# Attention probabilities divided ahead of the value product, which is turned round and packed in two column halves

## The chip, the cores and the metric

The kernel runs on one core of one Trainium2 chip. The metric is the device time of one execution in microseconds (us). Engines are TensorE (PE; PEld is its weight load), VectorE (DVE), ScalarE (ACT), GpSimd (POOL) and SyncE (SP, which issues the loads). All data are 32-bit floats. A product of the program shows as two passes in the trace, a turning (a transpose through TensorE) as one.

## What is computed

Two layers of a trunk on 384 tokens: 128 context tokens and 256 latent ones. A layer has three mixers that read one projection of the normalised tokens (latent attention, a gated linear scan, a state-space scan), whose gated sum is projected back, and a mixture of experts. The part that matters here is the attention of 16 heads and its output projection:

```python
def attend(q, k, v):
    ...
        s = jnp.einsum('bqhd,bkhd->bhqk', qblk, k).astype(jnp.float32) * scale
        p = jax.nn.softmax(s, axis=-1).astype(v.dtype)
        return jnp.einsum('bhqk,bkhd->bqhd', p, v)
...
    o_a = attend(q, k, v).reshape(Bsz, L, A_HEADS * A_V) @ P['a_wo'][l]
...
    merged = g[:, :, 0] * o_a + g[:, :, 1] * o_b + g[:, :, 2] * o_c
```

Context tokens read context keys alone; latent tokens read latent and context keys. Queries and keys have 96 columns per head, values 64.

## The kernel before, in words

Everything is written by hand: each engine has its own instruction list in a block, semaphores order them, and a block ends when all engines have ended theirs. The layer loop runs twice over the same blocks. The tokens are three tiles of 128; tile 0 is the context, tiles 1 and 2 are latent.

The attention block (TensorE code from line 846) goes through 48 steps, step i being head i // 3 and token tile i % 3. Tile 0 has one key tile, tiles 1 and 2 have three, so a step is 128 or 384 columns wide. A step is: scores on TensorE (line 873), the negated row maximum on VectorE (967), the exponential with its row sum on ScalarE (928), the turning of the probabilities on TensorE, one pass per key tile (882), their copy out of PSUM by VectorE (945), and the weighing of the values on TensorE (301, called from `weigh_values`), with the turned probabilities as weights and 64 value columns moving. Once per head, TensorE turns the queries and keys of the head after next (863, seven passes), ScalarE copies the queries (913) and VectorE the keys (938). Scores run AHEAD = 2 steps ahead of the turning; the probabilities have three buffers. Five PSUM banks rotate among scores, turned probabilities, queries and keys; three more collect the weighed values of eight heads per tile. After eight heads VectorE takes reciprocals of the row sums and scales the values out of PSUM (952, 954) into `o_tok`, tokens on partitions.

The next block makes the gate of this mixer (`W_GA`) and the output projection (`W_AO`). The projection needs features on partitions, so TensorE turns `o_tok` in 24 passes (`to_features`, line 333), VectorE copies it (497) into `oT`, and only then `feature_major` (301) runs. `gated_sum` multiplies the projection by the gate and writes the result to `mT`. Between these stand products of the modulation (380 in four quarters of the array's columns, 405 its small follow-up). Weight chunks pass through a ring of three, each loaded when the chunk three ahead of it has been read last. The block behind it begins the linear scan; there VectorE copies six decay tiles out of PSUM (1184).

What sets the order is the order of the lines below, engine by engine.

## Time and profile before

| what | value |
|---|---|
| median of three runs | 2664.28 us (2662.90 to 2666.83) |
| the profiled execution | 2660.27 us |
| its span, first to last instruction | 2658.3 us |
| TensorE busy | 2324.3 us, 87% of the span |
| VectorE busy | 828.9 us, 31% |
| ScalarE busy | 565.8 us, 21% |
| mean granted TensorE clock | 0.932 of full speed |

The busy shares are averages over stages with different limits, and matmuls are pipelined, so a busy TensorE is not one at its peak. A stage is read from its own stretch: who waits for whom there, and what a single head does in order of time. The attention stages begin at 229.4 and 1546.8 us.

### The profile page before, as it was taken

The numbers are of one execution on the slowest core, as the hardware profiler recorded it, in microseconds if no ns is written. First come the engines' busy times: TensorE is split into PE (matmuls) and PEld (weight loads), VectorE is DVE, ScalarE is ACT, GpSimd is POOL, SyncE is SP. The second block draws the span as 40 slices with busy tenths as digits, with TensorE's granted clock in tenths as the row PEclk, the third lists the DMA queues.
The fourth block names the chain that finished last, engine by engine and source line by source line (L and its number), as shares of the span: only waits on it lengthen the run. The fifth ranks groups of instructions, "written<-read, shape, count | busy, mean of one in ns | idle before, by whom it ended". The sixth has DMA issues, their size and how long they took to land. (4 is left out here: it accounts for less than half of the span.)

```text
span 2658.3 us, 35179 instructions
## 1 busy us (share of the span) xinstructions
PE 2324.3 (87%) x14554; PEld 1406.2 (53%) x14554; DVE 828.9 (31%) x1447; ACT 565.8 (21%) x1160; POOL 96.5 (4%) x64
## 2 busy tenths in 40 slices
PE   6999999999887988988479999999998779799873
PEld 3546754754555545555335466547545555455542
DVE  1255512530635222110203653125206452321002
ACT  2133301410244121000021332033102540210000
POOL 0000000100021000000000000001000210000000
PEclk8999998999988998998789999989999889899996
DMA  6321052214301215999553211331243102179993
GB/s 252 111 97 64 1 190 80 79 64 158 127 20 45 95 38 218 402 419 420 219 212 112 81 56 50 141 111 48 89 143 132 48 1 94 38 282 413 420 420 134
DMA packets 136274, 407.01 MB, mean 153 GB/s; under 512 B 9446, under 2 KB 34534, under 8 KB 125352
## 3 DMA queue, kind: packets, MB, share of 16 engines
q1 hardware_dynamic: 122600, 388.37, 38.4%
q10 hardware_dynamic: 11776, 9.97, 1.1%
q0 software_dynamic: 1728, 6.29, 0.7%
q8 instruction: 120, 1.97, 0.3%
q14 instruction: 50, 0.41, 0.0%
HBM read 388.59 MB, written 16.02 MB: 152 GB/s over the span
## 5 line engine op out<-in xcount | busy, mean ns | idle before, releaser
L301 PE MATMUL ps<-hT,ring 128*128 128x384 f32 x1344 | 473.3, 513 | 57.7 <-ACT arena L1524 30.6
L301 PEld LDWEIGHTS ps<-hT,ring 128*128 128x128 f32 x1344 | 268.0, 202 | 251.3 <-issue 84.1
L301 PE MATMUL ps<-ring,hT 128*128 128x512 f32 x768 | 337.1, 600 | 3.9 <-PEq L1033 3.9
L301 PE MATMUL ps<-arena,ring 128*128 128x384 f32 x768 | 253.0, 492 | 11.4 <-DVE arena L499 5.1
L301 PEld LDWEIGHTS ps<-ring,hT 128*128 128x128 f32 x768 | 147.1, 193 | 192.2 <-issue 191.6
L301 PEld LDWEIGHTS ps<-arena,ring 128*128 128x128 f32 x768 | 146.9, 192 | 115.4 <-issue 17.2
L1807 PE MATMUL ps<-ring,arena 128*32 128x256 f32 x2432 | 147.4, 405 | 30.3 <-DMA ring<-in_e_w 25.8
L1807 PE MATMUL ps<-arena 128*32 128x256 f32 x2432 | 143.9, 398 | 25.9 <-DMA arena<-in_e_w 25.9
L333 PE MATMUL ps<-cst,arena 128*128 128x128 f32 x472 | 77.6, 313 | 75.0 <-DVE arena L2086 34.4
L1807 PEld LDWEIGHTS ps<-ring,arena 128*32 128x32 f32 x2432 | 89.2, 117 | 85.0 <-issue 38.5
L1807 PEld LDWEIGHTS ps<-arena 128*32 128x32 f32 x2432 | 86.6, 115 | 78.7 <-issue 36.5
L2068 DVE TENSOR_TENSOR arena<-ps,arena 128x256 f32<-128x256 f32 (+1 forms) x44 | 17.1, 389 | 326.0 <-ACT arena L1917 326.0
L301 PE MATMUL ps<-ring,arena 128*128 128x384 f32 (+1 forms) x320 | 117.5, 528 | 0.0
L333 PEld LDWEIGHTS ps<-cst,arena 128*128 128x128 f32 x472 | 61.9, 160 | 102.4 <-DVE arena L2086 36.9
L301 PE MATMUL ps<-arena 128*128 128x64 f32 (+1 forms) x608 | 97.7, 295 | 1.5 <-DVE arena L945 1.4
L301 PEld LDWEIGHTS ps<-arena 128*128 128x128 f32 x608 | 87.8, 191 | 12.2 <-DVE arena L945 5.6
L301 PEld LDWEIGHTS ps<-ring,arena 128*128 128x128 f32 x320 | 60.6, 190 | 55.5 <-issue 30.6
L301 PE MATMUL ps<-mT,ring 128*128 128x384 f32 x256 | 83.1, 487 | 3.0 <-DVE arena L1665 3.0
L1917 ACT ACTIVATE arena<-ps 128x256 f32<-128x256 f32 (+1 forms) x44 | 15.7, 356 | 319.9 <-PE ps L1807 319.9
L301 PE MATMUL ps<-arena,mT 128*128 128x384 f32 x192 | 66.3, 509 | 15.7 <-DVE arena L2020 15.7
L1524 ACT ACTIVATE arena<-ps,arena 128x128 f32<-128x128 f32 x192 | 54.5, 366 | 73.2 <-DVE arena L1580 67.6
L1830 PE MATMUL ps<-arena 128*32 128x256 f32 x1216 | 68.8, 379 | 1.0 <-DVE arena L2077 1.0
(293 smaller groups left out, 2456.4 us busy)
## 6 DMA issues: line engine op xcount, KB each, us to landing
ring<-in_e_w SPq DMA_DIRECT2D x48, 2048.0 KB, 15.9
arena<-in_e_w SPq DMA_DIRECT2D x48, 2048.0 KB, 17.5
ring<-in_w_in SPq DMA_DIRECT2D x36, 2048.0 KB, 7.8
ring<-in_w_ada SPq DMA_DIRECT2D x24, 2048.0 KB, 8.1
ring<-in_a_wo SPq DMA_DIRECT2D x4, 2048.0 KB, 11.6
ring<-in_b_wo SPq DMA_DIRECT2D x4, 2048.0 KB, 8.1
ring<-in_c_wo SPq DMA_DIRECT2D x4, 2048.0 KB, 8.0
ring<-in_w_out SPq DMA_DIRECT2D x4, 2048.0 KB, 7.7
```

What stands on the lines that cost most here:

```text
L301: ins = pe.matmul(out, a, b, start=(i == 0), stop=(i == len(pairs) - 1))
L333: ins = pe.transpose(out[0:s.shape[1], i * P:i * P + P], s, ident)
L1524: ins = act.activation(diff[:, q % 2, P * i:P * i + P], bank(("ai", s, q))[:, P * i:P * i + P], ACT.Relu, bias=ex2[:, d, 0, h:h + 1], scal ...
L1807: ins = pe.matmul(out[32 * g:32 * g + 32], hc[:, e % 2, k, 32 * r:32 * r + 32], w[:, :, k, P * g:P * g + P], start=(k == 0), stop=(k == KD ...
L1830: ins = pe.matmul(out[32 * g:32 * g + 32], hidT[:, e % 2, r, 32 * k:32 * k + 32], w2[:, k, 256 * g:256 * g + 256], start=(k == 0), stop=(k ...
L1917: act.activation(sil[:, 2 * b:2 * b + n, :], bank(("w13", e, b))[:, 0:256 * n].rearrange("p (r i n) -> p r i n", i=2, n=P)[:, :, 0, :], AC ...
L2068: dve.tensor_tensor(hid[:, 2 * b:2 * b + n, :], bank(("w13", e, b))[:, 0:256 * n].rearrange("p (r i n) -> p r i n", i=2, n=P)[:, :, 1, :], ...
```

## The change

It does the following.

- The probabilities are divided by their row sum as soon as the exponential is done: VectorE takes the reciprocal of one column and multiplies the step's probabilities in place (`share_out`). TensorE's turning waits for that (`shared_out`).
- The copy of the turned probabilities moves from VectorE to ScalarE (`turned`), behind the exponential of three steps later and, once per head, the query copy. It goes to a buffer of three heads, in which the two latent tiles of one key tile lie side by side.
- The weighing is turned round: values are the weights (64 columns), turned probabilities move (128 columns for the context tile, 256 for both latent ones). Two heads go to columns 0 to 63 and 64 to 127 of the array. It is done once per pair of heads, behind the turning of the next pair's first step.
- A pair's result is copied once (`heads_out`) into `mT`, features on partitions already. So the turning of `o_tok` and its copies go, and the output projection reads `mT`. Its gated sum goes to `gated_a`, which VectorE copies to `mT` at the head of the next block.
- Scores run three steps ahead, probabilities have four buffers (two in `wsm`, which is not read any more at that time), six banks rotate, two hold pairs. The row sums and maxima lie in `rstd`.
- In the projection block, one small modulation product moves behind the first half of the output projection.

```diff
-            AHEAD = 2
-            B_PV, N_ROT = 5, 5
+            AHEAD = 3
+            B_PV, N_ROT, N_PV = 6, 6, 2
...
                     def turn_probs(i):
...
-                        pe.wait_ge(*read(("s", i)))
+                        pe.wait_ge(*following(pe, "shared_out"))
...
+                    def weigh_values(j):
+
+                        out = claim(pe, ("pv", j), B_PV + j % N_PV)
+                        for h in (2 * j, 2 * j + 1):
+                            for t in range(NT):
+                                pe.wait_ge(*read(("pt", NT * h + t)))
+                        for c in range(2):
+                            h = 2 * j + c
+                            pe.matmul(out[V_A * c:V_A * c + V_A, 0:P], v_a[:, 0, h, :], probsT[:, h % 3, 0:P], start=True, stop=True)
+                        for k in range(NKT - 1):
+                            for c in range(2):
+                                h = 2 * j + c
+                                ins = pe.matmul(out[V_A * c:V_A * c + V_A, P:T], v_a[:, 1 + k, h, :],
+                                                probsT[:, h % 3, P + 2 * P * k:P + 2 * P * (k + 1)],
+                                                start=(k == 0), stop=(k == NKT - 2))
+                        ins.then_inc(*makes(("pv", j)))
...
-                        if i >= 1:
-                            weigh_values(i - 1)
+                        if i >= 1 and i % (2 * NT) == 0:
+                            weigh_values(i // (2 * NT) - 1)
...
                         if j >= 0 and next_head(j):
                             queries(next_head(j))
+                        if j >= 0:
+                            turned(j)
...
+                    def share_out(i):
...
+                        dve.wait_ge(*read(("s", i)))
+                        r = rsum[:, t, h:h + 1]
+                        dve.reciprocal(r, r).then_inc(*counts("dve_step"))
+                        dve.wait_ge(*counted("dve_step"))
+                        dve.tensor_scalar(probs[i % 4][:, 0:n], probs[i % 4][:, 0:n], r, None, ALU.mult
+                                          ).then_inc(*counts("shared_out"))
...
-                    to_features(pe, "oa", o_tok)
+                    feature_major(pe, W_AO[0], ("ao", 0), mT)
                     modulation_features_pe(pe, ADA_FIRST + 1, rows_a[:, 1, :])
-                    project_pe(pe, W_AO, "ao", oT, "oa", lambda: modulation_pe(pe, ADA_FIRST + 2))
+                    modulation_pe(pe, ADA_FIRST + 2)
+                    feature_major(pe, W_AO[1], ("ao", 1), mT)
...
                 def _(dve):
+                    dve.tensor_copy(mT[:, :, :], gated_a).then_inc(*counts("dve_step"))
+                    dve.wait_ge(*counted("dve_step"))
```

On TensorE, in the middle of the attention, before. L873 are scores, L882 the turning of probabilities, L301 the weighing; a `psum_free` wait is for a reader of that PSUM bank.

```order
L882 MATMUL ps<-cst,arena 128x128 x2
L301 MATMUL ps<-arena 128x64 [waits psum_free0,psum_free6]
L301 MATMUL ps<-arena 128x64 x2
L873 MATMUL ps<-arena 128x384 [waits psum_free0]
L882 MATMUL ps<-cst,arena 128x128 [waits psum_free1,psum_free4]
L301 MATMUL ps<-arena 128x64 [waits psum_free4,psum_free7]
L301 MATMUL ps<-arena 128x64 x2
L873 MATMUL ps<-arena 128x128 [waits psum_free2,psum_free3]
```

Now, on TensorE at a pair's end. L893 and L897 are the weighing, in 64-column weights.

```order
L882 MATMUL ps<-cst,arena 128x128 [waits psum_free5,shared_out]
L882 MATMUL ps<-cst,arena 128x128 x2
L873 MATMUL ps<-arena 128x128 [waits psum_free0,psum_free4,psum_free3]
L882 MATMUL ps<-cst,wsm 128x128 [waits psum_free1,shared_out]
L893 MATMUL ps<-arena 64x128 [waits psum_free5,psum_free3,psum_free1,psum_free6]
L893 MATMUL ps<-arena 64x128
L897 MATMUL ps<-arena 64x256 x6
L873 MATMUL ps<-arena 128x384 [waits psum_free2]
```

The weighing of single steps has become one group per pair, and its first product waits for the readers of several banks, which are the copies of the turned probabilities; the next scores stand behind it.

On ScalarE at the same places, before. L928 is the exponential, L913 the query copy.

```order
L928 ACTIVATE arena<-ps,arena 128x384 [waits nmax_ready,psum_full4,psum_full3,psum_free2]
L913 ACTIVATE arena<-ps 96x384 [waits psum_full0,psum_free4]
L928 ACTIVATE arena<-ps,arena 128x384 [waits nmax_ready,psum_full3,psum_full2,psum_free0]
L928 ACTIVATE arena<-ps,arena 128x128 [waits nmax_ready,psum_full0,psum_full4,psum_free3]
L928 ACTIVATE arena<-ps,arena 128x384 [waits nmax_ready,psum_full2,psum_full1,psum_free0]
```

Now, on ScalarE. L947 is the exponential, L918 the query copy, L933 the copy of turned probabilities.

```order
L947 ACTIVATE arena,rstd<-ps,rstd 128x384 [waits psum_full2,nmax_ready,psum_full1]
L918 ACTIVATE arena<-ps 96x384 [waits psum_full3,psum_free2]
L933 ACTIVATE arena<-ps 128x3x128 [waits psum_full5,psum_free3]
L947 ACTIVATE arena,rstd<-ps,rstd 128x128 [waits psum_full0,nmax_ready,psum_full5]
L933 ACTIVATE arena<-ps 128x128 [waits psum_full1,psum_free0]
```

Each step's copy stands behind the exponential of the step three later, and at a head's end behind the query copy too; the exponential waits for VectorE's maximum (`nmax_ready`).

On VectorE, now, where a pair's output copy (L974) stands. L986 is the maximum, L967 and L969 the dividing, L959 the keys' copy.

```order
L967 RECIPROCAL rstd<-rstd 128x1 [waits psum_free0]
L969 TENSOR_SCALAR arena<-arena,rstd 128x128 [waits dve_step]
L974 COPY mT<-ps 128x384 [waits psum_full6]
L986 TENSOR_REDUCE rstd<-ps 128x1 [waits psum_full4,psum_free6]
L959 COPY arena<-ps 96x512 [waits psum_full0]
L967 RECIPROCAL rstd<-rstd 128x1 [waits psum_free2,psum_free0]
L969 TENSOR_SCALAR wsm<-wsm,rstd 128x384 [waits dve_step]
L986 TENSOR_REDUCE rstd<-ps 128x1 [waits psum_full2]
```

The copies of turned probabilities are gone from this engine; each step has a maximum and a dividing, one step behind it.

## Rows read from the trace of the kernel before

**Rows 1.** Waits, first attention stage: who waited, us, times, longest.

```profile
ACT arena L928 <- DVE arena L967: 34.7, 32, 1.8
DVE arena L967 <- PE ps L873: 14.8, 40, 0.6
```

**Rows 2.** Windows: length, busy PE, PEld, DVE, ACT, POOL, granted clock, DMA.

```profile
240.00:268.40 28.40, 28.40 (x209) 24.22 (x209) 20.84 (x44) 14.36 (x46) 0.00 (x0) 1.00 0.01 2
...
306.00:310.00 4.00, 1.69 (x14) 1.41 (x12) 3.13 (x7) 0.00 (x0) 0.00 (x0) 0.78 0.01 2
...
532.00:534.00 2.00, 0.10 (x1) 0.00 (x0) 2.00 (x2) 1.35 (x2) 2.00 (x1) 1.00 0.00 0
```

**Rows 3.** Timeline, one head of the attention: start, length, engine, line, operation.

```profile
263.07 0.86 PE L873 MATMUL ps<-arena 96*128 96x384 f32 x2
...
263.77 0.93 PE L863 MATMUL ps<-cst,arena 128*96 128x128 f32 x7
...
264.04 0.56 DVE L967 TENSOR_REDUCE arena<-ps 128x1 f32<-128x384 f32 x1 [0.38 <-PE ps L873]
...
264.77 0.58 ACT L928 ACTIVATE arena<-ps,arena 128x384 f32<-128x384 f32 x1 [1.01 <-DVE arena L967]
264.86 0.78 PE L301 MATMUL ps<-arena 128*128 128x64 f32 x6
...
265.47 0.49 ACT L913 ACTIVATE arena<-ps 96x384 f32<-96x384 f32 x1
265.48 0.86 PE L873 MATMUL ps<-arena 96*128 96x384 f32 x2
...
267.46 0.29 DVE L967 TENSOR_REDUCE arena<-ps 128x1 f32<-128x128 f32 x1 [0.25 <-PE ps L873]
...
268.39 0.93 PE L863 MATMUL ps<-cst,arena 128*96 128x128 f32 x7
```

**Rows 4.** Timeline, first and last instructions of the first attention stage.

```profile
229.42 1.70 PE L863 MATMUL ps<-cst,arena 128*96 128x128 f32 x14 [1.16 <-PEq L598]
...
234.12 0.33 PE L882 MATMUL ps<-cst,arena 128*128 128x128 f32 x1 [1.18 <-ACT arena L928]
...
309.42 0.69 DVE L954 TENSOR_TENSOR mT<-ps,arena 128x512 f32<-128x512 f32 x1
...
310.80 23.01 PE L301 MATMUL ps<-hT,ring 128*128 128x384 f32 x64 [2.64 <-PEq L846]
```

**Rows 5.** VectorE's groups by shape: count, busy us, mean ns, idle before.

```profile
L945 DVE COPY arena<-ps 128x384 f32<-128x384 f32 x64 | 35.7, 557 | 3.9 <-PE ps L882 2.9
...
L938 DVE COPY arena<-ps 96x512 f32<-96x512 f32 x32 | 22.0, 686 | 38.3 <-PE ps L863 34.4
...
L1403 DVE TENSOR_SCALAR arena<-arena,vec 128x388 f32<-128x388 f32 x24 | 10.2, 423 | 15.0 <-ACT arena L1365 14.5
...
L1184 DVE COPY arena<-ps 128x512 f32<-128x512 f32 x12 | 8.3, 692 | 13.8 <-PE ps L1038 13.8
...
L369 DVE TENSOR_SCALAR hT<-hT,amp,mod 128x128 f32<-128x128 f32 x12 | 4.1, 344 | 0.1
...
L1189 DVE TENSOR_SCALAR arena<-arena 128x3072 f32<-128x3072 f32 x2 | 3.5, 1759 | 0.1
...
L952 DVE RECIPROCAL arena<-arena 128x8 f32<-128x8 f32 x12 | 2.4, 203 | 0.4
```

**Rows 6.** Timeline of TensorE in the experts: products in four column quarters.

```profile
1046.45 10.57 PE L1807 MATMUL ps<-ring,arena 128*32 128x256 f32 x192 [2.41 <-DVE arena L2034]
```

**Rows 7.** Timeline of TensorE between gate and output projection.

```profile
356.33 0.95 PE L405 MATMUL ps<-fold,arena 128*128 128x2 f32 x8
...
357.21 1.92 PE L380 MATMUL ps<-ring,scond 128*32 128x512 f32 x16
...
359.07 2.84 PE L333 MATMUL ps<-cst,mT 128*128 128x128 f32 x24
...
364.67 20.88 PE L301 MATMUL ps<-arena,ring 128*128 128x384 f32 x64 [1.98 <-DVE arena L497]
```

More of the change, by code:

```diff
@@ L878, in turn_probs @@
                         k0, k1 = KEYS[t]
-                        pe.wait_ge(*read(("s", i)))
+                        pe.wait_ge(*following(pe, "shared_out"))
                         out = rotating(("pt", i))
                         for k in range(k1 - k0):
-                            ins = pe.transpose(out[:, P * k:P * k + P], probs[:, i % 3, P * k:P * k + P], ident)
+                            ins = pe.transpose(out[:, P * k:P * k + P], probs[i % 4][:, P * k:P * k + P], ident)
                         ins.then_inc(*makes(("pt", i)))
-                    def weigh_values(i):
-                        h, t = STEPS[i]
-                        k0, k1 = KEYS[t]
-                        if h % 8 == 0:
-                            claim(pe, ("pv", t, h // 8), B_PV + t)
-                        pe.wait_ge(*read(("pt", i)))
-                        c = V_A * (h % 8)
-                        ins = matmuls(pe, ps[:, B_PV + t, c:c + V_A],
-                                      [(probsT[:, i % 2, P * k:P * k + P], v_a[:, k0 + k, h, :]) for k in range(k1 - k0)])
-                        if h % 8 == 7:
-                            ins.then_inc(*makes(("pv", t, h // 8)))
+                    def weigh_values(j):
[13 more added lines that the diff above has]
+                        ins.then_inc(*makes(("pv", j)))
                     head(0)
@@ L914, in queries, with turned @@
                         act.wait_ge(*read(("qT", h)))
+                    def turned(i):
+                        h, t = STEPS[i]
+                        n = KEYS[t][1] - KEYS[t][0]
+                        act.wait_ge(*made(("pt", i)))
+                        if t == 0 and h >= 3:
+                            act.wait_ge(*made(("pv", (h - 3) // 2)))
+                        if t == 0:
+                            out = probsT[:, h % 3, 0:P]
+                            src = bank(("pt", i))[:, 0:P]
+                        else:
+                            out = probsT[:, h % 3, P:].rearrange("p (k q) -> p k q", q=2 * P)[:, :, P * (t - 1):P * t]
+                            src = quad(bank(("pt", i))[:, 0:T])
+                        act.activation(out, src, ACT.Copy).then_inc(*reads(("pt", i)))
                     queries(0)
@@ L970, in _ @@
                             keys(next_head(j))
-                        if 0 <= j < len(STEPS):
-                            turned(j)
-                        if j >= 2:
-                            h, t = STEPS[j - 2]
-                            if h % 8 == 7:
-                                heads_out(t, h // 8)
+                        if 0 <= j + AHEAD - 1 < len(STEPS):
+                            share_out(j + AHEAD - 1)
+                        if j >= 1 and (j - 1) % (2 * NT) == 0:
+                            heads_out((j - 1) // (2 * NT) - 1) if j > 1 else None
             with nc.Block() as block:
```

45 lines of the change are left out of this document (19 added, 26 removed).

## The prediction

> **What bounds the kernel now.** I read the waits of the attention stretch first, then its busy times by window, then the instructions of one head in order of time. In the waits, ScalarE waits for VectorE and VectorE for TensorE, while TensorE hardly waits for anybody [rows 1]. The window of the steady part says the same: TensorE is busy for all of its 28.4 us, VectorE for 20.84, ScalarE for 14.36, at full granted clock [rows 2]. One head (three steps) takes from the start of its seven turning passes at 263.77 us to the next such start at 268.39 us, 4.62 us, and in it TensorE goes from pass to pass [rows 3]; a pair of heads is 9.24 us. The stage takes from 229.42 to 310.80 us, 81.4 us [rows 4], twice in the run (once per layer). So only what shortens TensorE's queue without giving it a new wait can help here; VectorE, at three quarters, has about 1.2 us per head to spare.
>
> **The change part by part.**
>
> **Weighing (gain on TensorE).** Before, a step of three key tiles has six passes that take 0.62 us (264.86 to 265.48) [rows 3]; a head has fourteen, 1.45 us, a pair 2.9 us. Now a pair is 16 passes in two column halves: per half two of 128 and six of 256 columns, 1792 columns. A full-width pass costs 0.84 ns per column (64 passes of 384 columns in 20.88 us) [rows 7], so a half takes 1.51 us. Whether two halves run side by side no row shows; four quarters do: 192 passes of 256 columns took 10.57 us, 53 ns each [rows 6], a quarter of 256 x 0.84 ns. I take full overlap (nearest row). Leaving quarter mode cost 0.13 us: four rounds of 512 columns from 357.21 end at 358.94, the next pass starts at 359.07 [rows 7]. With entry, 0.2 us, so the weighing W of a pair takes 1.7 us, 1.2 less than before. The bounds are 1.6 (no entry cost) and 3.2 (no overlap at all).
>
> The Trainium skill, TensorEngine Tiling (Array Packing), section Tiling Modes, says that a change of tiling mode, not just of tile, drains the engine. A drain estimated from the score passes (two last 0.86 us, of which 2 x 0.32 is streaming) [rows 3] would be 0.2 us each way; W would be 1.9 us and the run 3 us longer, where the measured exit gives 0.13.
>
> **Dividing by the sum (cost on VectorE).** It takes the copy of the turned probabilities off VectorE (ScalarE gets it, and is half idle) and adds, per step, a reciprocal of one column and a multiplication in place. The first costs at most the 0.20 us of eight columns; the second 0.42 us for 384 columns, since the 388-column one with a per-partition factor is the same form; for 128 columns 0.34, from a two-factor one [rows 5]. With 0.03 us between instructions, a 384-wide step costs 0.68 us and a 128-wide one 0.60. The copies cost about 0.59 and 0.31. The maxima cost 0.56 and 0.29 us [rows 3], the keys' copy 0.69, a pair's output copy 0.56 [rows 5]. VectorE's sum per pair is then 4 x 0.59 + 2 x 0.32 + 2 x 0.72 + 4 x 0.68 + 2 x 0.60 + 0.59 = 8.95 us, just under the 9.24 us of a pair. It has no room left for a wait.
>
> **The new wait (the heart of the sum).** TensorE's weighing of a pair stands right behind the turning of the next pair's first step, and waits until all six turned steps are copied. The last copy (step 5) is on ScalarE behind the exponential of step 8 and a query copy; that exponential needs VectorE's maximum of step 8. Behind the weighing, on TensorE's queue, stand the scores of step 10, and VectorE's in-order queue stands still at the maximum of step 10. So VectorE cannot work during a weighing, and the weighing cannot start before VectorE has done the five maxima that follow the last one. I lay one period out from the start of a weighing:
> - weighing 1.70; scores of step 10 to their maximum 0.97 (263.07 to 264.04) [rows 3];
> - VectorE without a gap: maximum 10 (0.59), dividing 9 (0.60), output copy (0.59), maximum 11 (0.59), keys (0.72), dividing 10 (0.68), maximum 12 (0.32), dividing 11 (0.68), maximum 13 (0.59), dividing 12 (0.60), maximum 14 (0.56): 6.52;
> - maximum 14 to its exponential 0.17, exponential with its sum 0.70, query copy 0.53 [rows 3], copy of step 11 0.49 (the query copy's shape), TensorE's start 0.06: 1.95.
> Together 1.70 + 0.97 + 6.52 + 1.95 = 11.1 us per pair where it was 9.24. Within it TensorE's work (4.62 x 2 - 2.9 + 1.7 = 8.0 us) and ScalarE's fit. The third step of lead and the fourth buffer let scores and exponentials run ahead of the turning; neither stands in this chain. If the reciprocal took 0.15 us and the narrow multiplication 0.28 (estimates from the same rows, for one column and for half the slope), the period would be 10.8.
>
> **Start and end of the stage.** The first turning started at 234.12 us, just behind the first exponential [rows 4]. From there VectorE has dividing 0 to 6 and maxima 2 to 8 with one keys' copy ahead of the first weighing: 4 x 0.68 + 3 x 0.60 + 4 x 0.59 + 2 x 0.32 + 0.72 + 0.56 = 8.8 us, then 1.95: 244.9, which is 15.5 us after the start. Then six periods, 66.8 us. Behind the seventh weighing two steps are left: 1.70 + 0.97 + 2.34 (maximum, dividing, output copy, maximum) + 0.87 (exponential) + 0.68 (dividing) + 0.58 (turning, at 0.11 per pass, and 0.25 latency) + 0.55 (copy) + 1.95 (last weighing and its latency) + 0.56 (output copy) + 0.69 (change of stage, 310.11 to 310.80) = 10.9 us. Sum 93.2 us against 81.4: **11.8 us lost per layer**. The eight-head output copies that VectorE made before are inside the 81.4.
>
> **After the attention (gain).** The 24 turning passes and six copies between 359.07 and 364.67 us go, 5.6 us in which TensorE waited for VectorE at the end [rows 7]. Four small modulation products that ran under that wait now stand between the two projections: 0.95 us (the like group at 356.33) [rows 7]. Gain **4.6 us per layer**. The weight loads keep their order and are ahead.
>
> **The copy back (nothing).** VectorE copies 3072 columns at the head of the next stage. That costs about 1.76 us, by the scaling of the same size, and lies in the 13.8 us that VectorE idles ahead of the twelve copies there [rows 5]; only if that idle were gone would it cost its 1.8.
>
> **Sum.** Per layer 11.8 - 4.6 = 7.2 us, twice 14.4. The profiled execution took 2660.27 us (span 2658.3 and 2.0 around it), so 2674.7; it lies 4.0 us under the median of the three runs, 2664.28, so the forecast on that scale is 2678.7, **2679 us**, slower by 0.5%. Its own range is 2668 to 2692: the cheap dividing takes off 5 us, a clock that no longer falls at the stage's end (below) 4 more, and half a microsecond more per weighing or wait puts 8 to 13 on.
>
> **The rivals.**
> - **TensorE's relief wins (faster).** If the copy of step 5 were not late, the period would be VectorE's 8.95 us: per layer 8 x 0.29 + 4.6, and 1.6 for the output copies of eight heads, 8.5 us gained, 2647 us. For it: TensorE bounds today. Against it: the order on ScalarE is written out. It decides once a period is under 9.2 us. Chance 0.08.
> - **The wait is partly covered (same).** Four dividings in the chain, each 0.2 us cheaper, take 0.8 us off each period and 11 us off the run: 2668. Chance 0.12.
> - **The halves do not overlap.** W is 3.2 us; 16 weighings on the path cost 1.5 more each: 2703. No 64-column pass stands in the trace; the quarters speak against it. Chance 0.08.
> - **The clock falls.** TensorE now idles some 3 us of every 11, more than half of it close ahead of the weighing. The granted clock averaged 0.78 from 306 to 310 us, where the stage ran out in thin turning and weighing passes, but stayed at 1.00 from 532 to 534 us with TensorE nearly idle [rows 2]. Each fall to the 1.2 GHz level ahead of a weighing costs its 1.5 us and the scores' 0.65 again, 2.1: eight falls of 16 make 2696, all 2713. Chance 0.18.
>
> The Trainium skill, TensorE: Matmul & The Clock Gate, Part 4: PE-mode transpose, says that turning passes do not count as activity for the clock in the way products do. By that rule the stretch ahead of a weighing, mostly turning passes and idle, would look idle, which speaks for this last rival. The 306 to 310 row agrees; the 532 to 534 row neither excludes nor shows it.
>
> **How the numbers follow.** Forecast 0.54, clock 0.18, the same 0.12, faster 0.08, no overlap 0.08. A measurement here tells about 0.2% from no change, that is 2659 to 2669.6. Faster 0.08, same 0.12, slower 0.80. The range leaves out the faster case, part of the same and the clock's upper half: 2666 to 2704.
>
> **What would show it.** In the changed profile: TensorE's wait at the weighing (source line 893) for ScalarE's copies, about 2 us with the two small gaps ahead of it, eight times per layer; VectorE's maxima waiting some 2.5 us for the scores behind each weighing; starts of weighings 11.1 us apart; 16 passes of a weighing in 1.5 to 1.7 us; the attention 93 us long; the output projection starting straight after the second modulation product. Starts under 9.2 us apart make the prediction wrong, and so does a weighing that waits for nothing.

## The result and the profile after

On one chip the kernel before took 2665.83 us (median of 7 runs, 2662.90 to 2668.76) and the changed one 2674.23 us (7 runs, 2670.93 to 2675.19): **1.003 times the time before, interval 1.002 to 1.004**, 0.3% slower. The forecast was 2679, range 2666 to 2704. The profiled execution took 2675.19 us.

The page of the changed kernel, busy us and share of the span (before: TensorE 2324.3 us, ScalarE 565.8 us):

```profile
span 2673.4 us, 34806 instructions
...
PE 2302.5 (86%) x14314; PEld 1367.3 (51%) x14314; DVE 822.9 (31%) x1525; ACT 602.8 (23%) x1256; POOL 96.0 (4%) x64
```

TensorE has 22 us less to do and the run is 8 us longer. The waits from 240 to 305 us, inside the first attention stage (who waited, for whom, us in total, times, longest), answer to [rows 1]:

```profile
DVE rstd L986 <- PE ps L873: 17.4, 18, 1.9
...
PE ps L873 <- ACT arena L918: 13.4, 12, 1.3
ACT wsm L947 <- DVE rstd L986: 11.2, 16, 2.2
...
PEld ps L893 <- issue: 1.3, 6, 0.2
```

TensorE now waits 13.4 us, twelve times, at one place: the scores of a head's first step (L873) wait for ScalarE's query copy (L918). At the weighing (L893) it waits for next to nothing (0.2 us each time), and the prediction had named that as a sign of being wrong. VectorE's maxima wait for scores, and ScalarE for the maxima. One period, from one weighing to the next, in order of time (start, length, engine, line, idle before and who ended it) answers to [rows 3]:

```profile
254.04 0.49 ACT L933 ACTIVATE arena<-ps 128x384 f32<-128x384 f32 x1
...
254.06 0.49 PE L873 MATMUL ps<-arena 96*128 96x128 f32 x2 [0.93 <-ACT arena L918]
...
254.67 0.44 PE L893 MATMUL ps<-arena 128*64 128x128 f32 x4
...
254.91 1.49 PE L897 MATMUL ps<-arena 128*64 128x256 f32 x12
...
256.34 0.91 PE L873 MATMUL ps<-arena 96*128 96x384 f32 x2
...
257.29 0.56 DVE L986 TENSOR_REDUCE rstd<-ps 128x1 f32<-128x384 f32 x1 [1.89 <-PE ps L873]
...
258.73 0.56 DVE L986 TENSOR_REDUCE rstd<-ps 128x1 f32<-128x384 f32 x1
...
259.21 0.68 DVE L959 COPY arena<-ps 96x512 f32<-96x512 f32 x1
...
260.08 0.49 ACT L918 ACTIVATE arena<-ps 96x384 f32<-96x384 f32 x1
...
260.62 0.49 PE L873 MATMUL ps<-arena 96*128 96x128 f32 x2 [1.30 <-ACT arena L918]
...
261.14 0.29 DVE L986 TENSOR_REDUCE rstd<-ps 128x1 f32<-128x128 f32 x1 [0.60 <-PE ps L873]
...
262.88 0.56 DVE L986 TENSOR_REDUCE rstd<-ps 128x1 f32<-128x384 f32 x1
...
264.87 0.49 PE L873 MATMUL ps<-arena 96*128 96x128 f32 x2 [0.93 <-ACT arena L918]
...
265.48 0.44 PE L893 MATMUL ps<-arena 128*64 128x128 f32 x4
```

Weighings start 10.81 us apart (254.67 to 265.48; forecast 11.1; a pair before, 9.24). The sixteen passes end in the next scores after 1.67 us. The copy that the weighing needs, L933 at 254.04, ends at 254.53, and at that time TensorE is just through with the late first scores and their turning. Both conditions fall together, so the wait shows at the scores and not at the weighing. The period adds up as 1.67 (weighing) + 0.95 (scores to their maximum) + 6.15 (VectorE from maximum 10, at 257.29, to the end of maximum 14) + 2.04 (from there to the next weighing).

VectorE's groups by shape in the first attention stage (count, busy us, mean ns, idle before) answer to [rows 5]:

```profile
L967 DVE RECIPROCAL rstd<-rstd 128x1 f32<-128x1 f32 x48 | 7.5, 156 | 2.0 <-ACT arena L947 1.2 <-ACT wsm L947 0.3
L969 DVE TENSOR_SCALAR arena<-arena,rstd 128x384 f32<-128x384 f32 x16 | 6.7, 420 | 0.6
...
L969 DVE TENSOR_SCALAR arena<-arena,rstd 128x128 f32<-128x128 f32 x8 | 2.3, 287 | 0.3
```

Windows of the changed kernel (length, busy time of PE, PEld, DVE, ACT, POOL, granted clock, DMA share, GB/s) answer to [rows 2]; the last is the end of layer 2's stage:

```profile
243.86:308.70 64.84, 51.38 (x336) 36.13 (x337) 44.16 (x127) 41.88 (x120) 0.00 (x0) 1.00 0.01 1
...
1568.00:1630.00 62.00, 49.44 (x324) 34.78 (x324) 42.04 (x121) 39.18 (x114) 0.00 (x0) 1.00 0.00 1
...
1640.00:1648.00 8.00, 6.19 (x21) 3.58 (x22) 0.56 (x1) 1.65 (x2) 0.00 (x0) 0.50 0.01 2
```

TensorE is busy 79% of the attention and keeps the 2.4 GHz level through the periods of both layers, until the last step of layer 2. TensorE's timeline behind the stages answers to [rows 4] and [rows 7]:

```profile
319.05 20.88 PE L301 MATMUL ps<-hT,ring 128*128 128x384 f32 x64 [1.29 <-PEq L846]
...
363.34 1.92 PE L380 MATMUL ps<-ring,scond 128*32 128x512 f32 x16
365.19 3.17 PE L301 MATMUL ps<-mT,ring 128*128 128x384 f32 x9
...
1640.96 2.81 PE L897 MATMUL ps<-arena 128*64 128x256 f32 x12
1645.07 23.01 PE L301 MATMUL ps<-hT,ring 128*128 128x384 f32 x64 [1.29 <-PEq L846]
```

The stages take 229.09 to 319.05 us, 89.96, and 1553.28 to 1645.07 us, 91.79 (before 81.4; forecast 93.2). The output projection follows the second modulation product at once. In layer 1 the gate projection takes 20.88 us, where before it took 23.01 [rows 4] at a granted clock of 0.50 in its first 3.2 us:

```profile
310.80:314.00 3.20, 3.20 (x5) 1.82 (x6) 0.00 (x0) 1.10 (x1) 0.00 (x0) 0.50 0.00 0
```

In layer 2 the clock was at 0.50 from 1640 us on, and the last weighing's passes took 2.81 us instead of 1.49.

So the two profiled executions, whose spans are 15.1 us apart, differ by these stretches (us, the changed kernel's less before's, layer 1 / layer 2); the stretches ahead of the attention are 1.1 us shorter:

| stretch | forecast | measured |
|---|---|---|
| attention | +11.8 / +11.8 | +8.6 / +10.4 |
| from there to the low-rank gate products | -4.6 / -4.6 | -6.9 / -4.8 |
| from there to the router | 0 / 0 | -2.1 / -2.5 |
| router to the last turning of the experts | 0 / 0 | +3.6 / +2.2 |
| last turning to the next layer's first modulation product | 0 | +4.3 |
| last turning to the turning of the output, and that itself | 0 | +4.0 |

Down to the router the change is worth about +2.7 us in both layers together. Some 14 us arise where no line was changed. (The medians are 8.4 us apart: the profiled execution of before was shorter than its median, that of the changed kernel longer.) The experiments therefore had two questions: what sets the 10.81 us, and where those 14 us come from. Each ratio is to executions of the kernel before that were taken together with that kernel's, and times of different kernels are compared through it.

| kernel | median us | ratio to before, interval | period us |
|---|---|---|---|
| e1_heads_earlier | 2667.62 | 1.0002 (0.9991 to 1.0012) | 10.54 |
| e2_weigh_later | 2667.64 | 1.0011 (1.0001 to 1.0020) | 10.42 |
| e3_both | 2650.85 | 0.9950 (0.9933 to 0.9967) | 9.08 |
| e4_weigh_twice | 2696.79 | 1.0116 (1.0090 to 1.0142) | 12.33 |
| e5_no_scaling | 2665.81 | 0.9996 (0.9986 to 1.0006) | 10.48 |
| e6_two_ahead | 2667.01 | 0.9998 (0.9987 to 1.0009) | 9.95 |
| e7_query_first | 2664.55 | 0.9998 (0.9988 to 1.0007) | 10.15 |
| e10_code_as_before | 2671.43 | 1.0021 (1.0012 to 1.0031) | 10.81 |
| e11_before_31_more | 2673.24 | 1.0024 (1.0015 to 1.0034) | as before |
| e13_both_query_first_code | 2642.64 | 0.9913 (0.9896 to 0.9929) | 8.93 |
| e15_code_hidden | 2638.48 | 0.9911 (0.9892 to 0.9929) | 8.93 |

### The profile page after: what moved, and what is told of

Same layout as the page of the kernel before. It is cut to its first block and busy times, and to the rows that moved or that the text cites. A ratio compares the mean times of both kernels' runs of the same rounds, so it can differ in the third digit from the quotient of the medians.

```text
span 2673.4 us, 34806 instructions
## 1 busy us (share of the span) xinstructions
PE 2302.5 (86%) x14314; PEld 1367.3 (51%) x14314; DVE 822.9 (31%) x1525; ACT 602.8 (23%) x1256; POOL 96.0 (4%) x64
## 3 DMA queue, kind: packets, MB, share of 16 engines
q0 software_dynamic: 1728, 6.29, 0.7%
q8 instruction: 120, 1.97, 0.3%
## 5 line engine op out<-in xcount | busy, mean ns | idle before, releaser
L301 PE MATMUL ps<-hT,ring 128*128 128x384 f32 x1344 | 470.7, 511 | 55.0 <-ACT arena L1546 30.6
L301 PEld LDWEIGHTS ps<-hT,ring 128*128 128x128 f32 x1344 | 266.6, 201 | 248.4 <-issue 80.3
L301 PE MATMUL ps<-ring,hT 128*128 128x512 f32 x768 | 336.8, 599 | 3.9 <-PEq L1053 3.9
L301 PEld LDWEIGHTS ps<-ring,hT 128*128 128x128 f32 x768 | 147.0, 192 | 192.0 <-issue 191.4
L301 PE MATMUL ps<-arena,ring 128*128 128x384 f32 x512 | 169.5, 494 | 7.5 <-DVE arena L499 5.1
L301 PE MATMUL ps<-mT,ring 128*128 128x384 f32 x512 | 166.7, 487 | 3.0 <-DVE arena L1687 3.0
L301 PEld LDWEIGHTS ps<-arena,ring 128*128 128x128 f32 x512 | 98.6, 193 | 76.8 <-issue 11.5
L301 PEld LDWEIGHTS ps<-mT,ring 128*128 128x128 f32 x512 | 96.8, 190 | 73.8 <-DVE arena L1687 4.2
L301 PE MATMUL ps<-ring,arena 128*128 128x384 f32 (+1 forms) x320 | 117.5, 528 | 0.0
L873 PE MATMUL ps<-arena 96*128 96x384 f32 (+1 forms) x192 | 66.9, 439 | 31.6 <-ACT arena L918 31.5
L301 PEld LDWEIGHTS ps<-ring,arena 128*128 128x128 f32 x320 | 60.6, 190 | 55.5 <-issue 30.6
L301 PE MATMUL ps<-arena,mT 128*128 128x384 f32 x192 | 66.4, 510 | 15.7 <-DVE arena L2042 15.7
L1546 ACT ACTIVATE arena<-ps,arena 128x128 f32<-128x128 f32 x192 | 54.3, 365 | 73.4 <-DVE arena L1602 67.8
## 6 DMA issues: line engine op xcount, KB each, us to landing
ring<-in_a_wo SPq DMA_DIRECT2D x4, 2048.0 KB, 11.1
```

What stands on the lines that cost most here:

```text
L301: ins = pe.matmul(out, a, b, start=(i == 0), stop=(i == len(pairs) - 1))
L873: pe.matmul(out[:, 0:P * (k1 - k0)], head_qT[0:QK, h % 2, tok(t)], head_kT[0:QK, h % 2, P * k0:P * k1], start=True, stop=True).then_inc(*m ...
L1546: ins = act.activation(diff[:, q % 2, P * i:P * i + P], bank(("ai", s, q))[:, P * i:P * i + P], ACT.Relu, bias=ex2[:, d, 0, h:h + 1], scal ...
```

## Experiments: what sets the period

**The projection a step earlier (e1).** TensorE projects the next head, and ScalarE and VectorE copy it, one step earlier.

```diff
-                    return (i + 1) // NT + 1 if i % NT == NT - 1 and (i + 1) // NT + 1 < H_A else None
+                    return i // NT + 2 if i % NT == 1 and i // NT + 2 < H_A else None
```

> Queries and keys of a head are turned and copied one step earlier, all else as in the changed kernel. Theory A (a chain through the engines' orders: weighing, scores, VectorE's maxima, exponential, query copy, next head's first scores, next weighing): TensorE's waits for the query copy (1.3 and 0.9 us per pair of heads) go, the copy of the last turned step is reached 0.5 us earlier, and the starts of weighings go from 10.8 to about 9.6 us apart; some 17 us off the run, 2657 us. Theory B (VectorE is full since it divides): the period stays at 10.5 or more and the run within 3 us of the changed kernel's 2674.

The period came to 10.54 us, not 9.6, and the run to 2667.62 us, between the two theories: the period is as B had it, the run is not. TensorE's timeline of one period:

```profile
262.99 0.49 PE L873 MATMUL ps<-arena 96*128 96x128 f32 x2 [0.28 <-ACT arena L918]
...
264.69 0.44 PE L893 MATMUL ps<-arena 128*64 128x128 f32 x4 [1.10 <-ACT arena L933]
```

The wait at the first scores went from 0.93 to 0.28 us, and 1.10 us came up at the weighing, for the copy of the turned probabilities. That is the wait that the prediction named. In the changed kernel it is hidden behind the other one.

**The weighing a step later (e2).** It stands behind the turning of the next pair's second step, and the pair's output copy a step later too.

```diff
-                        if i >= 1 and i % (2 * NT) == 0:
-                            weigh_values(i // (2 * NT) - 1)
+                        if i >= 2 * NT and i % (2 * NT) == 1 or i == len(STEPS):
+                            weigh_values((i - 1) // (2 * NT) - 1 if i < len(STEPS) else H_A // 2 - 1)
```

> A pair is weighed one step later, so that the scores of one more step are made ahead of it; its output copy follows one step later too. Theory A: VectorE's 1.9 us wait for scores behind each weighing goes, the waits for the query copy stay; period about 9.8 us, 14 us off, 2660 us. Theory B: as the changed kernel, 2674 within 3 us.

10.42 us and a run of 2667.64, again between A and B. Of each pair's waits at the first scores 0.83 and 1.10 us stay. One of the two conditions was taken away and the other stood.

**Both (e3).**

> Both moves: heads turned one step earlier and pairs weighed one step later. Theory A: neither wait is left; the period falls to what TensorE (8.0 us of passes per pair) and VectorE (about 7.5) need, 8.5 to 9.2 us; 25 us off the changed kernel, about 2649 us, faster than the kernel before. Theory B: no better than 2670.

2650.85 us, 23.4 less than the changed kernel, where the two alone give 6.6 each; the period falls by 1.73 us, where the two alone give 0.27 and 0.39. This is what two waits that fall together look like: either alone is worth little. A window of this kernel:

```profile
243.00:300.00 57.00, 54.00 (x355) 36.50 (x354) 43.34 (x130) 43.08 (x127) 0.00 (x0) 1.00 0.01 1
```

TensorE is busy 95% of it. At 9.08 us per pair the stage is under the 9.24 of before.

**The query copy first (e7).** On ScalarE alone, the query copy moves ahead of the exponential of its step.

```diff
+                        if j >= 0 and next_head(j):
+                            queries(next_head(j))
                         if i < len(STEPS):
...
-                        if j >= 0 and next_head(j):
-                            queries(next_head(j))
```

> The changed kernel with one line moved on ScalarE alone: the query copy of the next head stands ahead of the exponential of the same step instead of behind it. Everything on TensorE and VectorE keeps its order. Theory A (the wait for the query copy is only where the chain from weighing to weighing shows; behind it stand the copies of the turned probabilities that the weighing needs): the wait of the first scores falls from 0.93 and 1.30 us to under 0.7, but a wait for the last copy appears at the weighing, and the period falls only a little, to 10.3 to 10.7; the run to 2666 to 2672. Rival B (the query copy behind the exponential is the whole of the cause): the period falls by the two waits, 2.2 us, to about 8.7, and the run by some 35 us to 2640.

The waits came as theory A says (0.67 and 0.50 us at the first scores, 0.48 at the weighing). The period, 10.15 us, and the run, 2664.55, are a little shorter than it had them:

```profile
263.55 0.46 PE L873 MATMUL ps<-arena 96*128 96x128 f32 x2 [0.50 <-ACT arena L918]
...
264.60 0.44 PE L893 MATMUL ps<-arena 128*64 128x128 f32 x4 [0.48 <-ACT arena L933]
```

**Two steps of lead (e6).**

```diff
-            AHEAD = 3
+            AHEAD = 2
```

> The changed kernel with two steps of lead instead of three; the four buffers stay. Theory A (the third step of lead covers the way scores, maximum, exponential, reciprocal, multiplication, turning, which is longer than before): with two steps TensorE waits for the multiplication at the turnings, most of all behind each weighing; that way takes 0.95 + 0.45 + 0.65 + 0.2 + 0.45 = 2.7 us against some 1.6 us of work on TensorE per step, two steps ahead 3.2 less the weighing's standstill: the period grows by 0.5 to 2 us, the run by 8 to 32 us, to 2682 to 2706. Rival B (the third step only puts the scores of a head's first step right behind its own query copy; with two there is a step more between projection and scores): the wait of 0.93 and 1.30 us for the query copy goes, the period falls to about 9.8 and the run to about 2658.

Rival B had the direction. The period falls to 9.95 us and no first scores wait any more. The run, 2667.01, is 9 us above what B gave: the stage falls to 86.42 us only, since its first weighing comes 1.1 us later after its start and its end is 0.5 us longer. TensorE's groups of the stage show a smaller wait instead, for the dividing (L969) at the turnings, 10.5 us per layer:

```profile
L873 PE MATMUL ps<-arena 96*128 96x384 f32 (+1 forms) x96 | 33.8, 437 | 0.2
...
L882 PE MATMUL ps<-cst,arena 128*128 128x128 f32 x56 | 11.2, 294 | 5.9 <-DVE arena L969 5.9
L882 PE MATMUL ps<-cst,wsm 128*128 128x128 f32 x56 | 10.8, 286 | 4.7 <-DVE wsm L969 4.6
```

So in this order the third step of lead, which the change added, costs more than it covers. With it a head's first scores stand directly behind that head's own projection, with an exponential between projection and query copy on ScalarE. Whether two steps would be better beside the moves of e3 too was not run.

**The weighing twice (e4).** All products of a pair are done twice, the second time over the first.

```diff
-                        for c in range(2):
...
-                        for k in range(NKT - 1):
+                        for k in [None, 0, 1, 2, None, 0, 1, 2]:
```

> Each pair is weighed twice over, with the same result. Theory A (the weighing lies on the chain): 16 weighings longer by 1.5 us each, 24 us on, 2698 us, period 12.3 us. Rival C (the weighing fills time in which TensorE waits anyway): under 5 us on, period 11.0 or less.

2696.79 us, 22.6 more than the changed kernel for 16 times 1.5 us, and a period of 12.33, longer by 1.52. The weighing is on the path to its full length, as the prediction had it. TensorE's timeline, with the scores behind the doubled weighing:

```profile
256.43 0.44 PE L895 MATMUL ps<-arena 128*64 128x128 f32 x4
...
257.96 0.42 PE L895 MATMUL ps<-arena 128*64 128x128 f32 x4
...
259.61 0.91 PE L873 MATMUL ps<-arena 96*128 96x384 f32 x2
```

From first pass to scores 3.18 us against 1.67: the second set costs 1.51, which is the streaming time of one half. The other 0.16 us is what a weighing takes beyond it from its first pass to the scores behind it; going into half mode comes ahead of the first pass and is not in it. In e3, where the copies that the weighing needs are done 0.7 us ahead of it, three turning passes start 0.42 us ahead of a weighing (261.53 to 261.95) and 0.33 us ahead of scores (264.36 to 264.69), so going in costs some 0.09 us, and in and out together about 0.25.

**No scaling (e5).**

```diff
-                        dve.reciprocal(r, r).then_inc(*counts("dve_step"))
-                        dve.wait_ge(*counted("dve_step"))
-                        dve.tensor_scalar(probs[i % 4][:, 0:n], probs[i % 4][:, 0:n], r, None, ALU.mult
-                                          ).then_inc(*counts("shared_out"))
+                        dve.reciprocal(r, r).then_inc(*counts("shared_out"))
```

> The changed kernel without the multiplication of the probabilities by the reciprocal (the reciprocal stays); its outputs are then not divided by the sums, so it leaves out part of the computation. Theory A (VectorE's dividing lies in the chain between two weighings): in the changed kernel a multiplication stands 0.29 or 0.42 us after its reciprocal, and four of 0.29 + 0.42 + 0.29 or 0.42 stand between the maximum behind a weighing and the last maximum ahead of the next; where ScalarE's exponential then waits for a maximum that comes up to 0.4 us earlier twice or three times per pair, the period falls from 10.81 by 0.8 to 1.4 us, to 9.4 to 10.0, and the run by 12 to 22 us, to 2652 to 2662. Rival B (the chain goes through scores, exponential and query copy, and VectorE's multiplications fall into its own waiting, 1.9 us behind each weighing and 0.4 to 0.6 ahead of three maxima): the period stays above 10.5 and the run at 2668 or more.

The period falls by 0.33 us, to 10.48, and the run to 2665.81, both just below what B had and far from A. The stages shorten by 3.4 and 5.2 us, of which some 1.8 in layer 2 is the fall of the clock in the changed kernel's profile. The first scores still wait for the query copy (window of 240 to 305 us, 13.4 in the changed kernel):

```profile
PE ps L873 <- ACT arena L918: 11.4, 12, 1.0
```

So taking away the 2.2 us of multiplications per pair gains a seventh of them: beside VectorE's chain lies one through ScalarE's exponentials and copies and the first scores, nearly as long. As with the two waits above, this does not tell what the dividing would be worth with that other chain out of the way. The forecast had the whole dividing, four times 0.60 to 0.68, in the chain.

## Experiments: the time outside the attention

**The kernel before once more.**

> The kernel before, profiled once more, to see what repeats of the 15 us between the two profiled executions that lies outside the attention. Theory A (the turn of the loop between the layers, and the expert stage's waits for weights, are longer in the changed kernel by its own doing): from the last turning of layer 1 to the first modulation product of layer 2 it is again about 25 us (29 to 30 in five profiles of changed kernels), from the second router to the end 344 to 346 (350 to 354). Rival B (they vary from execution to execution): about 29 and about 350.

Theory A. From the last turning (1315.64) to the first modulation product (1340.35) it was 24.71 us, and from the second router to the end 344.67. In the profiles of the changed kernel and of e1 to e7 the turn took 29.2 to 29.8. It is no accident of one execution.

The stretch with the change in it does vary. From the attention's start to the router the kernel before took 755.3 and 755.4 us in its first profile, 758.9 and 757.8 in this one, 759.1 and 758.9 in that of e11 below, whose code there is the same; the changed kernel took 754.9 and 758.5, and e10 below, with the changed kernel's attention, 755.6 and 754.7. So the +2.7 us is within what executions of one kernel differ by: down to the router the change costs nothing that can be told. Nor does the clock's fall in layer 2 come with the change; in e10 that gate projection is

```profile
1642.54 20.88 PE L301 MATMUL ps<-hT,ring 128*128 128x384 f32 x64 [1.29 <-PEq L846]
```

**The code's length.** The trace holds 120 transfers on a queue called instruction, 1.97 MB, that is 16.4 KB each: twice, up to whole pieces, TensorE's code of 987,264 bytes (972,864 in the changed kernel). At the turn of the loop all engines, but for VectorE's and ScalarE's last 2 to 4 us, stand still while the next modulation weights are loaded. The next two kernels change the length of TensorE's code and nothing else, by instructions that wait for a semaphore set long ago (two such waits share one instruction of 64 bytes). The first gives the changed kernel the length of before, the second gives the kernel before the length of the changed one and 16,384 bytes.

```diff
+                    for _ in range(110):
+                        pe.wait_ge(*read(("pv", 0)))
                     pe.wait_ge(*following(pe, "h_ready", 2))
...
+                    for _ in range(140):
+                        pe.wait_ge(*read("parts"))
                     pe.wait_ge(*following(pe, "chosen_ready"))
...
+                    for _ in range(200):
+                        pe.wait_ge(*read("parts"))
                     for g in range(2):
                         pe.wait_ge(*following(pe, "picked"))
```

The changed kernel with before's length (e10):

> The changed kernel with 225 more TensorE instructions in the loop, which only wait for semaphores that were set long ago, at three places around the router where TensorE waits for other engines anyway (4.96, 5.08 and 7.83 us). TensorE's code is then as long as in the kernel before (987,264 bytes; changed: 972,864). In seven profiles of changed kernels the turn of the loop (last turning to first modulation product) took 29.2 to 29.8 us against 25.1 and 24.7 in two profiles of the kernel before, and between the loads of the modulation weights and the restart three transfers of 16 KB of code stood in the trace against two; at the end of the run 19.9 us against 16.8, two such transfers against one. Theory A (where the code ends against the pieces in which it is fetched sets this): the turn takes 25 us again and the end 16.8, the run is 8 to 15 us shorter than the changed kernel, 2659 to 2666, plus up to 3 us where the waiting instructions are not hidden. Rival B (it is something else in the changed kernel, say the order of its transfers): 29 and 19.9 stay, 2674 to 2680.

The kernel before with 31 instructions more, 62 such waits ahead of the last of these places (e11):

> The kernel before with 31 more TensorE instructions in the loop that only wait for a semaphore set long ago, where TensorE waits 7.8 us for VectorE at the router. Its TensorE code is then 989,248 bytes, which is the changed kernel's length and one piece of 16,384 bytes. Theory A (the place of the code's end against the pieces of 16 KB): the turn of the loop takes 29 us where it took 25, the end 19.9 where it took 16.8, the expert stage some 3 us more per layer: 7.7 to 14 us slower than the kernel before, 2674 to 2680. Rival B: no difference, 2664 to 2668.

For each of the four kernels: TensorE's first product of layer 2 (in brackets how long it had idled), the code transfers between the issue of the weight loads and that product, and TensorE's first product behind the loop. The kernel before:

```profile
1337.03 6.33 PE L392 MATMUL ps<-ring,scond 128*32 128x512 f32 x32 [23.15 <-issue]
...
q8 instruction: 2, 0.03, 1.1%
...
2646.70 4.33 PE L333 MATMUL ps<-cst,xT 128*128 128x128 f32 x24 [14.88 <-PEq L556]
```

The changed kernel:

```profile
1344.23 4.50 PE L392 MATMUL ps<-ring,scond 128*32 128x512 f32 x20 [27.46 <-issue]
...
q8 instruction: 3, 0.05, 1.0%
...
2661.55 5.25 PE L333 MATMUL ps<-cst,xT 128*128 128x128 f32 x24 [17.95 <-PEq L556]
```

The changed kernel with before's length:

```profile
1342.32 6.19 PE L392 MATMUL ps<-ring,scond 128*32 128x512 f32 x32 [23.06 <-issue]
...
q8 instruction: 2, 0.03, 1.1%
...
2655.63 5.38 PE L333 MATMUL ps<-cst,xT 128*128 128x128 f32 x24 [14.92 <-PEq L556]
```

The kernel before with 31 instructions more:

```profile
1348.67 6.29 PE L392 MATMUL ps<-ring,scond 128*32 128x512 f32 x32 [27.35 <-issue]
...
q8 instruction: 3, 0.05, 1.0%
...
2664.57 4.58 PE L333 MATMUL ps<-cst,xT 128*128 128x128 f32 x24 [17.94 <-PEq L556]
```

In these four kernels both waits go with the length and not with the rest of the change: 23.15 and 23.06 us with two transfers, 27.46 and 27.35 with three; 14.88 and 14.92 at the end, against 17.95 and 17.94. At the turn the third piece comes with the weight loads on the same DMA engines (6.29 MB moved before the restart, 5.38 with two pieces). **31 instructions that do nothing, hidden in a wait, make the kernel before 1.0024 times as long (1.0015 to 1.0034), 6.4 us.** The two waits add 7.3 us; the instructions themselves are hidden, for the first expert is through 73.1 us after the router with and without them. That is most of the 1.003 of the change. Giving the changed kernel before's length brought both waits back, but the run only to 2671.43 us, above the 2659 to 2669 expected. Something about its added instructions is not hidden: its first expert is through 77.5 us after the router instead of 73.5, in both layers. Without those 8 us its 2671.43 would be about 2663, an estimate. Only two places of the code's end against the 16 KB pieces were tried, so what other lengths give stays open.

Of the experts' own time a part follows the length too, in layer 1: from the first expert's turning to the last turning 254.1 and 254.0 us in the two profiles of before, 256.9 with 31 instructions more, 257.4 in the changed kernel, 253.8 with before's length. In layer 2 it does not: 256.7 in the changed kernel, but 254.7 with the 31 instructions. That part stays open.

**All moves together (e13, e15).** The projection earlier, the weighing later, the query copy first, and the waiting instructions.

> The changed kernel with the projection of the next head a step earlier, the weighing a step later, the query copy ahead of the exponential of its step, and the 225 waiting instructions. Theory A: the stage is then at TensorE's own work, a period of 8.0 to 9.0 us (9.08 without the query copy's move), and the turn of the loop at 25 us: 2650.9 of the two moves together, less 8 to 15, less up to 8: 2628 to 2643. Rival B (neither of the two new edits adds to the two moves): 2648 to 2655.

2642.64 us, at the upper end of A. A window, for comparison with that of the two moves alone:

```profile
243.00:300.00 57.00, 55.28 (x360) 36.86 (x359) 44.35 (x134) 43.57 (x130) 0.00 (x0) 1.00 0.01 1
```

TensorE is busy 97%. The last kernel puts the waiting instructions elsewhere: 55 and 45 at the first two places, 125 ahead of the experts' last turnings.

> The three moves of the last kernel (projection earlier, weighing later, query copy first) with the same 225 waiting instructions at other places: 55 and 45 of them ahead of the router's products and ahead of the placing (TensorE waits 4.96 and 5.08 us there), 125 ahead of the last turnings of the expert stage, where TensorE waits 13.3 us for VectorE; none ahead of the dispatch, where the 100 put the experts 4 us later per layer. Theory A (the code's end against the pieces of 16 KB sets the turn and the end, and the waiting instructions cost only where TensorE does not wait longer than they take): the turn stays at 25 us, the end at 16.9, the first expert starts 4 us earlier per layer, and the run is 2634 to 2640, the upper end if the expert stage hangs on the place of its own code, which is 8,000 bytes short of the kernel before. Rival B (the 4 us were no cost of the waiting instructions): 2642 or more.

2638.48 us, as A has it: **0.9911 times the time before (0.9892 to 0.9929), better than both kernels.** The turn takes 24.74 us, the first expert is through after 73.4 us, so at that place the 4 us per layer did come from the added instructions. In the whole run the gain over e13 is not shown: that one stood at 0.9913. The traces show one reason: in layer 2 the experts take 257.1 us for e13's 252.8, which takes the 4 us back there, for a reason that stays open.

## Why the prediction was right, and where it was not

- **Direction and size.** The time lies in the range, slower as forecast. The sum, +14.4 us, measured +8.4. But its parts are not the ones forecast: up to the router the change costs between nothing and 3 us instead of 14, and the rest goes in the main with the code's length, on which the prediction has no word. The attention did become slower, by 8.6 us per layer, but the stretches behind it took that back. That the whole run came out slower, and by this order, is luck.
- **Weighing.** W was forecast at 1.7 us with full overlap of the halves; 1.67 measured, and the doubled weighing shows all of it on the path. The rival without overlap (3.2 us) is out. The Trainium skill, TensorEngine Tiling (Array Packing), section Tiling Modes, says that a change of mode drains the engine. The trace agrees that it costs something, 0.16 us behind the first pass and some 0.09 ahead of it, less than the 0.4 that the drain was estimated at. (In the prediction's quarter-mode row, 10.57 us over 192 passes is 55 ns each, not 53; nothing changes by it.)
- **VectorE's chain: the term that was mis-sized.** "VectorE without a gap ... 6.52" was 6.15 us from maximum 10 (257.29) to the end of maximum 14, of which 0.60 is a wait for scores, so 5.55 of work. The reciprocal took 0.156 us, not 0.20, and the multiplication of 128 columns 0.287, not 0.34. Instructions that follow each other also start earlier than their lengths say: maximum 11 begins at 258.73 with 0.56, the next copy at 259.21.
- **Where the wait stands: the step that failed.** "TensorE's wait at the weighing (source line 893) for ScalarE's copies, about 2 us" is next to nothing, and "a weighing that waits for nothing" was the prediction's own sign of being wrong. TensorE waits at L873 instead, 0.93 and 1.30 us per pair. The prediction has no wait of a head's first scores for the query copy; it counts that copy only in ScalarE's tail ahead of the weighing. That tail was right in length, 2.04 us for 1.95, and the wait it stands for is there, 1.10 us, once the other is taken away (e1). The first scores ahead of the weighing do little harm of their own, since the weighing's copies come at the same time (e1, e7). Those in the middle of the pair are the 0.60 us in VectorE's chain. So it was not VectorE without a gap that ran from weighing to weighing, but a way that changes over to ScalarE's query copy and the first scores and back.
- **The third step of lead.** "Neither stands in this chain" is wrong for the lead: without its third step the period is 0.86 us shorter (e6). The fourth buffer was not tried.
- **The period** of 11.1 came to 10.81, by 1.0 less work of VectorE and 0.6 of a wait not foreseen. The prediction's variant with a cheap dividing gives 10.8 as well, and its two prices, 0.15 and 0.28 us, were right; that it meets the period is luck, since it takes off 0.3 us of work and has no wait. The maxima wait 1.89 us for scores behind the weighing, where 2.5 was forecast.
- **Stage and what follows.** 93.2 us was 89.96 and 91.79. In layer 1 start and end were each some 0.6 to 0.7 us shorter than laid out. Layer 2's 91.79 belongs to that execution: with the same attention e10 took 89.96 and 90.22. The gain of 4.6 us behind the attention was 4.8 in layer 2, where the clock was as before: the output projection starts as forecast, and the copy of 3072 columns delays nothing. The 2.1 and 2.5 us from the low-rank gate products to the router were not forecast; in layer 1, 1.7 of them are these products themselves, 8.02 us for 9.75.
- **The rival of the dividing ("same").** It took four dividings to be 0.2 us cheaper each and 11 us off the run. Taking all multiplications away gives 8 us, 0.33 us of each period. VectorE's dividing alone is hardly what the period hangs on.
- **The clock.** The rival with falls ahead of each weighing did not come: 1.00 in both windows. The Trainium skill, TensorE: Matmul & The Clock Gate, Part 4: PE-mode transpose, says that turning passes do not count as activity for the clock in the way that products do. In this stage, which has turnings and waits in every period, the granted clock stayed at the upper level all the same. It fell only at the end of layer 2's stage, where before it fell in both layers. The change does keep the clock up there as a rule, worth 2.1 us per layer in the gate projection: that took 23.0 to 23.5 us in all six layers of three profiles with the attention of before, and 20.88 us in twenty of the 22 layers of the eleven profiles with the change in them. The two others are layer 2 of the changed kernel's profile, 23.01, and layer 1 of e3's, 22.51; why these fell, no run settles. The prediction had these 4 us in its range, not in its sum.
- **Faster.** The rival put its point of decision at 9.2 us per period. The moves of e3 reach 9.08, and the run is faster. But that threshold was too strict: at 9.95 and 10.15 us per period e6 and e7 already take as long as the kernel before (0.9998), with the longer turn of the loop in them.

## What to carry to other kernels

When a wait has two conditions that end together, taking one away shows little; look at the queue one instruction further, and move both. A lead of more steps is no gain in itself: look which copies stand between a projection and its first use. And before a difference of a few microseconds is explained by the edited stage, compare the unchanged ones: the length of the code alone moved this kernel by 0.24%, and one stretch of 755 us by up to 3.8 us from execution to execution.

## What the runs showed of the hardware

TensorE's code comes in pieces of 16 KB during the run (120 transfers). How many stand ahead of the restart at a loop's turn went with the code's length in the four kernels compared: two or three here, 25 or 29 us with weight loads beside them, and one or two behind the loop, 16.8 or 19.9 us without. Products in two halves of the array run side by side: two times 1792 columns in 1.51 us, with about 0.25 us for both changes of mode.
